# Attention by pairs of heads: half-array matmuls, probabilities divided before the transposes

## What is computed

```
def attend(q, k, v, scale):
    s = jnp.einsum('bhqd,bhkd->bhqk', q, k).astype(jnp.float32) * scale
    p = jax.nn.softmax(s, axis=-1).astype(v.dtype)
    return jnp.einsum('bhqk,bhkd->bhqd', p, v)
...
        s_win = jnp.einsum('bhqd,bhrkd->bhqrk', q_row, k_band).astype(f32) * scale + bias
        s_ctx = jnp.einsum('bhqd,bhcd->bhqc', q_row, kc).astype(f32) * scale
```

## Time and profile before

| | us |
|---|---|
| median of 3 runs | 1773.76 |
| lowest and highest | 1771.92, 1777.18 |
| the profiled execution, whole | 1772.61 |
| its span on the core | 1770.9 |

### The profile page before, as it was taken

One profiled execution on the slowest core, in us unless ns is written; L12 is line 12 of the kernel. 1 busy time (PEld: TensorE's weight loads), 2 busy tenths in 40 slices (PEclk: granted clock), 3 DMA queues, 4 the chain that ended last, 5 costly groups with the idle time before them and its releaser, 6 DMA issues.

```text
span 1770.9 us, 24625 instructions
## 1 busy us (share of the span) xinstructions
PE 1637.0 (92%) x9536; PEld 1383.1 (78%) x9536; DVE 992.3 (56%) x1739; ACT 759.2 (43%) x1470; POOL 670.4 (38%) x389
## 2 busy tenths in 40 slices
PE   7998989899999989899999998978899988889998
PEld 3876769766877668688888886967897876789998
DVE  5855825855275545359596964134136385546655
ACT  4333654344544443442323234247444644454443
POOL 0532334611343002355454553534551551133442
...
GB/s 336 198 141 78 201 92 166 176 39 1 98 96 183 26 102 92 51 143 143 142 191 166 285 167 119 66 95 79 155 96 48 93 140 96 99 133 193 178 188 119
DMA packets 69851, 230.63 MB, mean 130 GB/s; under 512 B 18280, under 2 KB 24808, under 8 KB 56424
## 3 DMA queue, kind: packets, MB, share of 16 engines
...
HBM read 216.45 MB, written 12.58 MB: 129 GB/s over the span
## 4 chain that ended last, share of the span: by engine, by line
PE 74%; DVE 10%; ACT 7%; issue 3%; POOL 3%; DMA 1%; ACTq 0%; POOLq 0%; DVEq 0%; SPq 0%
PE bank L1747 37%; PE bank L1829 9%; PE bank L1785 8%; PE bank L1767 4%; PE bank L2114 4%; PE bank L2093 3%; PE bank L1811 2%; PE bank L2100 2%; ACT wH L776 2%; POOL wL L663 1%; DVE mjunk L1204 1%; PE bank L1978 1%; DVE arena L1275 1%; POOL wL L665 1%; DVE acc L1207 1%
## 5 line engine op out<-in xcount | busy, mean ns | idle before, releaser
L663 POOL TENSOR_TENSOR wL<-raw,wH 128x1280 fp32r<-128x1280 f32 (+3 forms) x146 | 302.7, 2073 | 556.4 <-ACT wH L776 556.4
L665 POOL TENSOR_TENSOR wL<-raw,wH 128x768 fp32r<-128x768 f32 (+3 forms) x198 | 329.1, 1662 | 368.2 <-ACT wH L776 368.2
L776 ACT ACTIVATE wH<-raw 128x768 fp32r<-128x768 f32 (+6 forms) x396 | 296.7, 806 | 395.6 <-PE bank L1747 295.5
L1747 PE MATMUL bank<-hH,wH 128*128 128x512 f32 (+1 forms) x720 | 248.8, 346 | 5.2 <-DVE wL L1189 3.2
L1747 PE MATMUL bank<-hH,wL 128*128 128x512 f32 (+1 forms) x720 | 245.5, 341 | 0.0
L1747 PE MATMUL bank<-hL,wH 128*128 128x512 f32 (+1 forms) x720 | 245.4, 341 | 0.0
L1747 PE MATMUL bank<-oH,wH 128*128 128x512 f32 (+1 forms) x576 | 196.6, 341 | 2.9 <-DVE oL L1611 2.9
L1747 PE MATMUL bank<-oL,wH 128*128 128x512 f32 (+1 forms) x576 | 195.3, 339 | 0.0
L1747 PE MATMUL bank<-oH,wL 128*128 128x512 f32 (+1 forms) x576 | 195.2, 339 | 0.0
L1207 DVE SCALAR_TENSOR_TENSOR acc<-acc,cb 128x1024 f32<-128x1024 f32 x88 | 168.7, 1930 | 2.5
L1747 PEld LDWEIGHTS bank<-hH,wH 128*128 128x128 f32 x720 | 137.3, 191 | 22.8 <-DVE wL L1189 3.8
...
## 6 DMA issues: line engine op xcount, KB each, us to landing
...
```

Of the source, the lines that this page charges most:

```text
L663: pool.tensor_tensor(l_[:, 0:cut], r_[:, 0:cut], h_[:, 0:cut].bitcast(F32), ALU.subtract)
L665: pool.tensor_tensor(l_[:, cut:k * w], r_[:, cut:k * w], h_[:, cut:k * w].bitcast(F32), ALU.subtract)\
L776: act.activation(flat(wH, n)[:, part], flat(raw, n)[:, part], ACT.Copy)\
L1747: ins = pe.matmul(dst, w_[:, kk, c:c + P], r_[:, kk, lo:TOK], start=kk == k0 and m == 0, stop=kk == k0 + kn - 1 and m == 2)
```

## The change

Two heads that stand side by side in one group of 128 features make one step: 16 steps in layer 0, 8 in layer 1, plus 2 to drain. For `na`, `a_q` is no longer padded: the scores of the even head use partitions 0 to 63 and those of the odd head 64 to 127, in pieces of 128 keys that alternate between the two heads and their banks 4 and 5. VectorE divides the probabilities in SBUF (`pn`) before they are transposed. Then the values are stationary (64 columns) and the transposed probabilities move, so that the output comes out feature by token, the two heads in the two halves of the partitions of one bank; the transposes of the output, `s_o` and its division are gone. ScalarE rounds each pair's 128x128 output to `oH`, and VectorE writes `oL`. Probabilities have four buffers. The biases of the 512-key `na` scores are added in one instruction, with 256 zeros for the context keys. The scores of the next pair wait for the maximum where the scores were moved to SBUF (`na`, 512 keys), otherwise for Exp. Side work is spread anew by `side_done`, its last 12 matmuls in the first draining step. The first `na` block of each layer becomes `SHARED`. GpSimd's memset before the `na` phase is 256 wide instead of 4096. In the diff the three old loops (lines 1067 to 1099, 1575 to 1618 and 2079 to 2129 above) are left out, as are some old lines that one new line replaces.

```diff
+def head_pairs(l):
+    return [(qi, t, g) for qi, t in enumerate(att_tiles(l)) for g in range(HEADS // 2)]
...
+        a_q, a_k, a_v, a_tb = view(0, 4, TOK), view(2048, 4, TOK), view(4096, 4, 512), view(8192, 8, 6, 64)
+        A_ZERO, A_TB = 7936, 8192
...
+        s_pt = view(13824, 2, 512)
+        s_probs = dict(na=[view(at, 512) for at in (6144, 6656, 7168, 12800)],
+                       mla=[view(at, 512) for at in (12800, 13312, 10240, 10752)])
...
+        SHARED = [name in ("to", "wo") or (name == "ml" and j < 2) or (name, j) == ("na", 0) or (name, l) == ("ff", 1) for name, l, j in KEYS]
...
+        def side_done(br, l, s):
+            n = len(head_pairs(l))
+            if br == "na" and s == 0:
+                return 0
+            return KC * 12 if s >= n else (KC - 1) * 12 * (s + 1) // n
+        def side_step(br, l, c):
+            return next(s for s in range(len(head_pairs(l)) + 1) if side_done(br, l, s) >= 12 * c + 12)
...
-                pool.memset(a_q, 0.0).then_inc(S(f"na{l}_zero").handle, 1)
-                low_to(reach(N["ns", l, KC - 1]))
-                low_to(reach(N["ms", l, KC - 1]))
+                pool.memset(view(A_ZERO, CTX), 0.0).then_inc(S(f"na{l}_zero").handle, 1)
+                for br, last_used, side_name in (("na", ("na", l, 5), "ns"), ("mla", ("gate", l, GATES - 1), "ms")):
+                    low_to(reach(N[last_used]))
+                    turns = head_pairs(l)
+                    for s in range(len(turns) + 2):
+                        for c in range(KC):
+                            if side_step(br, l, c) + 1 == s:
+                                low_to(reach(N[side_name, l, c]))
+                    end()
...
-                            act.wait_ge(*S(tag + "zero").at(1))
-                            for up in range(2):
-                                r = slice(64 * up, 64 * up + 64)
-                                for tt in range(ntl):
-                                    src = tb[r, tt * 256:tt * 256 + 256].rearrange("p (a t) -> p a t", a=2)
-                                    dst = a_q[r, h0 + up:h0 + 4:2, (t + tt) * P:(t + tt) * P + P]
-                                    ins = act.activation(dst, src, ACT.Copy, scale=gcols[r, 0:1])
+                            for tt in range(ntl):
+                                src = tb[:, tt * 256:tt * 256 + 256].rearrange("p (a t) -> p a t", a=2)
+                                dst = a_q[:, h0 // 2:h0 // 2 + 2, (t + tt) * P:(t + tt) * P + P]
+                                ins = act.activation(dst, src, ACT.Copy, scale=gcols[:, 0:1])
...
+                    turns = head_pairs(l)
+                    for s in range(len(turns) + 2):
+                        if s >= 2:
+                            _, t, g = turns[s - 2]
+                            act.wait_ge(*S(tag + "o").at(s - 1))
+                            act.activation(oH[:, (4 if br == "na" else 0) + g, t * P:t * P + P], bank[s % 2][:, 0:P], ACT.Copy)\
+                                .then_inc(S(tag + "oH").up(1), 1)
+                        if 1 <= s <= len(turns):
+                            nk = att_keys(turns[s - 1][1]) * P
+                            for i in range(2):
+                                k = 2 * s - 2 + i
+                                act.wait_ge(*S(tag + "pt").at(k + 1))
+                                if s >= 2:
+                                    act.wait_ge(*S(tag + "o").at(s - 1))
+                                act.activation(s_pt[:, i, 0:nk], bank[6 + i][:, 0:nk], ACT.Copy).then_inc(S(tag + "pts").up(1), 1)
+                        if s < len(turns):
+                            qi, t, g = turns[s]
                             nk = att_keys(t) * P
+                            for i in range(2):
+                                k = 2 * s + i
+                                probs = s_probs[br][k % 4][:, 0:nk]
+                                act.wait_ge(*S(tag + "max").at(k + 1))
+                                if k >= 4:
+                                    act.wait_ge(*S(tag + "pt").at(k - 3))
+                                act.activation(probs, probs if br == "na" and t >= 2 else bank[4 + i][:, 0:nk], ACT.Exp,
+                                               bias=stat[:, 16 + k % 4:17 + k % 4],
+                                               accum_out=stat[:, 20 + k % 4:21 + k % 4]).then_inc(S(tag + "p").up(1), 1)
                         for c in range(KC):
+                            if side_step(br, l, c) + 1 == s:
                                 ahead(N["ns" if br == "na" else "ms", l, c])
...
+                share_ahead(N["gate", l, gate_range(l, "last").stop - 1])
...
+                    turns = head_pairs(l)
+                    def attended(s):
+                        if s >= 2:
+                            _, t, g = turns[s - 2]
+                            c, cols_ = (4 if br == "na" else 0) + g, slice(t * P, t * P + P)
+                            dve.wait_ge(*S(tag + "oH").at(s - 1))
+                            dve.tensor_tensor(oL[:, c, cols_], bank[s % 2][:, 0:P], oH[:, c, cols_].bitcast(F32),
+                                              ALU.subtract).then_inc(S(tag + "oL").up(1), 1)
+                    for s in range(len(turns) + 2):
+                        for k in (2 * s - 2, 2 * s - 1) if 1 <= s <= len(turns) else ():
+                            dve.wait_ge(*S(tag + "p").at(k + 1))
+                            link(dve.reciprocal(stat[:, 24 + k % 4:25 + k % 4], stat[:, 20 + k % 4:21 + k % 4]))
+                            probs = s_probs[br][k % 4][:, 0:att_keys(turns[s - 1][1]) * P]
+                            dve.tensor_scalar(probs, probs, stat[:, 24 + k % 4:25 + k % 4], None, ALU.mult)\
+                                .then_inc(S(tag + "pn").up(1), 1)
+                        for c in range(KC):
+                            if side_step(br, l, c) + 1 == s:
+                                branch_out(br, l, c)
+                            if br == "mla" and c < KC - 1 and side_step(br, l, c) + 2 == s:
+                                share_ahead(N["ms", l, c])
+                        for i in range(2 if s < len(turns) else 0):
+                            qi, t, g = turns[s]
+                            k, h, nk = 2 * s + i, 2 * g + i, att_keys(t) * P
+                            src = bank[4 + i][:, 0:nk]
+                            dve.wait_ge(*S(tag + "s").at(k + 1))
+                            if k >= 4:
+                                dve.wait_ge(*S(tag + "p").at(k - 3))
                             if br == "na" and t >= 2:
+                                if k >= 4:
+                                    dve.wait_ge(*S(tag + "pt").at(k - 3))
+                                step = A_TB + (h * 6 + (2 if t == 2 else 0)) * GRID_W - A_ZERO
+                                bias = view(A_ZERO, 2, step)[:, :, 0:CTX]
+                                scores = s_probs[br][k % 4]
+                                link(dve.tensor_tensor(scores.rearrange("p (a w) -> p a w", a=2),
+                                                       src.rearrange("p (a w) -> p a w", a=2), bias, ALU.add))
+                                src = scores
+                            dve.reduce_max(stat[:, 16 + k % 4:17 + k % 4], src, axis=AX,
+                                           negate=True).then_inc(S(tag + "max").up(1), 1)
+                            if i == 0:
+                                attended(s)
+                        if s >= len(turns):
+                            attended(s)
...
+                    turns = head_pairs(l)
+                    for s in range(len(turns) + 2):
+                        if s < len(turns):
+                            qi, t, g = turns[s]
+                            if s:
+                                moved = br == "na" and turns[s - 1][1] >= 2
+                                pe.wait_ge(*S(tag + ("max" if moved else "p")).at(2 * s))
                             if br == "na":
+                                for c in range(att_keys(t)):
+                                    for i in range(2):
+                                        r = slice(64 * i, 64 * i + 64)
+                                        ins = pe.matmul(bank[4 + i][:, c * P:c * P + P], a_q[r, g, t * P:t * P + P],
+                                                        a_k[r, g, c * P:c * P + P], start=True, stop=True)
+                                        if c == att_keys(t) - 1:
+                                            ins.then_inc(S(tag + "s").up(1), 1)
                             else:
+                                for i in range(2):
+                                    nk = att_keys(t) * P
+                                    pe.matmul(bank[4 + i][:, 0:nk], l_q[0:MLA_D, 2 * g + i, t * P:t * P + P],
+                                              l_k[0:MLA_D, 2 * g + i, 0:nk], start=True, stop=True).then_inc(S(tag + "s").up(1), 1)
+                        if s >= 2:
```

(21 more changed lines are left out.)

136 lines of the change are left out of this document (8 added, 128 removed).

## The result

| | before | after |
|---|---|---|
| median of the first comparison, us | 1773.99 | 1726.58 |
| lowest and highest of the four runs | 1771.92, 1777.18 | 1723.77, 1731.03 |
| the profiled execution, and its span | 1772.61, 1770.9 | 1731.03, 1729.3 |

The ratio is .9734, 95% interval .9708 to .9759: some 47 us less. In a second comparison, with five runs, it was .9731 (.9717 to .9744), 1729.15 against 1776.83. The profiled execution is 4.4 above the median of the first, so terms read from its trace add up to -41.6 and not to -47.4.

What follows compares the result with a forecast made beforehand. It took the Exp-to-Exp periods of the four attention loops as the bound, TensorE having no gap with 512 keys. Loops, ends and the rest summed to -45.8 from 1772.6, giving 1727 us; own range 1712 to 1739, 8 in 10 1708 to 1768.

Steps and rivals of the forecast that it cites:

- loops, layer 0: neighbourhood, latent: First to last Exp in layer 0: neighbourhood 86.9 to 65.2 us (-21.7), latent 83.8 to 75.3 (-8.5).
- loops, layer 1: neighbourhood, latent: First to last Exp in layer 1: neighbourhood 47.7 to 37.4 us (-10.3), latent 48.2 to 43.0 (-5.2).
- end of latent, layer 1: Stretch after layer 1's last latent Exp: 7.15 us becomes 10.4, +3.2, through a late gate tile.
- first projection, two layers: Wait for GpSimd before each layer's first projection shrinks by 2.35 us, -4.7 in all.
- Periods: Exp-to-Exp time per head pair: latent 6.2 us with 512 keys, 3.7 with 256; neighbourhood 5.1 to 5.2 and 3.4.
- The unknown price: Half-array matmul in scores and values: taken as .067 us side by side, 1.07 for 16 values; 1.71 in a row.
- the array empties at each change of shape: Rival, chance .12: TensorE drains when matmul shape changes, .2 us each, 120 changes, +24 us, 1751.
- One after the other: Rival, chance .22: half-array matmuls in the attention loops run in sequence, 16 values 1.71 us, scores 1.82; total 1755.
- The late gate tile: Layer 1's latent end: gate tile load queued behind the first wo block, which waits for VectorE's weight share; landing 5.1 us.
- The share on VectorE: First neighbourhood weight block: VectorE takes part of GpSimd's conversion, so the second piece starts 2.35 us earlier per layer.
- VectorE-bound: Neighbourhood pairs with 512 keys: VectorE, without gaps, sets the period of 5.1 to 5.2 us.
- The clock: Rival, chance .08: TensorE gaps within attention pairs bring the lower clock, 1.2 GHz; 130 us for all 48 pairs, 1857.

Runs made afterwards that it cites:

- The kernel that is this rival: Changed kernel with neighbourhood scores and all loops' values issued head by head, not alternating between array halves: 1741.96 us, ratio .9804.

## Why the prediction was right, and where it was not

**The sum.** 1727 against 1726.58 (1729.15 later). The terms, from the profiled executions:

| term | forecast | measured |
|---|---|---|
| loops, layer 0: neighbourhood, latent | -21.7, -8.5 | -21.4, -10.7 |
| loops, layer 1: neighbourhood, latent | -10.3, -5.2 | -11.5, -4.5 |
| end of neighbourhood, layer 0 | +1.0 | +1.4 |
| end of latent, layer 1 | +3.2 | +5.5 |
| other two ends | 0 | -.2 |
| first projection, two layers | -4.7 | -1.4 in each |

The last Exp to the first projection took 6.3 in place of 4.9 at the first end, 12.6 in place of 7.15 at the second. The measured terms make -44.2 of the profiled -41.6. The other 2.6 is not in any of them, nor were the query copies (-1.6) and the weight conversions behind Exp (+2) taken apart.

The mechanisms came as forecast, but that the sum hits to within 1 us is in part luck: the loops gave 2.4 more than forecast (-48.1 for -45.7), the ends and the first projection 4.4 less (+3.9 for -.5), and the profiled execution is itself 4.4 above the median. The working has three slips that changed nothing: 7 x 3.4 + 8 x 5.2 is 65.4 and not 65.2, 7 x 3.7 + 8 x 6.2 is 75.5 and not 75.3, and the terms of the latent end make 10.65 and not 10.4.

**Periods: right.** 6.11 for 6.2, 3.74 for 3.7, 3.33 for 3.4. Neighbourhood with 512 keys came to 34.2/7 = 4.9 on average in layer 0 and 5.0 in layer 1 for 5.1 to 5.2 (the expectations above have 5.09, which counts the two Exps of a pair into it), but my one number hides four cases: 4.5 without a side tile, 5.0 with one (4.7 in layer 1, where a tile is half as wide), 5.8 and 6.2 where GpSimd is in the way, and 5.7 in the second pair of layer 1, where TensorE makes up the side work of two pairs.

**The unknown price: right in sum, wrong in its parts.** I took .067 for a half-array matmul, so 1.07 for 16, and gave the drain a chance of its own, .12, as something that would come on top of the forecast or not. Measured are 1.02 for the values, and they hold both: 16 x .053 = .85, the lower bound, and .17 of drain; on the way into them scores lose another .2. So "I take .067" was too dear by .2 a pair, and "the array empties at each change of shape" was true, at .17 and not .2, though nowhere shown by the rows of before: the change from 128 to 64 stationary columns in the earlier trace rows has no gap, and I let it speak against the drain. Two errors of .2 to .4 a pair cancelled.

**One after the other: right for one half, wrong between the two.** The rival's 1755 went by 1.71 for sixteen values and 1.82 for sixteen scores. The kernel that is this rival ran at 1741.96, with 1.34 and 1.44 (1.51 and 1.64, less the gap at the change). The .107 was right for one half (.109 measured); what failed in "one after the other they go by their 128 moving columns, .107 each" is "one after the other", since the second half's instructions began four places early. With 256 keys that covers the whole row, so the rival's 4.0 and 4.1 were 3.75 and 3.34; with 512 its 6.8 and 5.85 were 6.59 and 5.3 to 5.5.

**The late gate tile: right, too small.** Its place in the queue was as told. The block in front of it waited for VectorE's share as I had it, but then .6 us more for GpSimd's part of the same weight block, which ends at 1472.49. Of the 12.6 us, 3.9 lie before the tile's issue (I had 4.35), 1.3 behind its landing (1.2). The term that was mis-sized is "landing 5.1": from 1473.27 to VectorE's start at 1480.68 it took 7.4, 2.3 more than in the earlier trace rows.

The block of weights in front is not the reason, though I took it for one: the tile stood behind it in the earlier trace rows too (issued at 1514.29 and 1514.72), and in layer 0 of the changed kernel, where it landed in 5.1. What differs is ScalarE's load of 1024 KB. It was issued at 1516.63 in the kernel before, behind both; now it is under way first, since the tile has moved behind it:

```profile
arena<-g_spill SPq DMA_DIRECT2D x1, 128.0 KB, 5.0
...
arena<-g_spill SPq DMA_DIRECT2D x1, 128.0 KB, 7.3
```

(kernel before, changed kernel; size, us to landing.) In the nine profiles that have the tile behind the block, it landed in 5.6 to 7.5 us in layer 1, with this load first, and in 4.9 to 5.4 in layer 0, with this load last. No run moved this load alone, so the reason is read from rows and not shown by an edit.

The clock behind the wait needed no term: in the kernel before, the first 4 us of `wo` were granted .50 too, and from the first `wo` matmul to the end both kernels took 247.3.

```profile
1523.65:1527.65 4.00, 4.00 (x19) 4.00 (x20) 1.98 (x5) 2.00 (x7) 0.00 (x0) 0.50 0.02 4
```

**The share on VectorE: too large.** "The second piece starts some 2.35 earlier" nearly held: counted from ScalarE's first conversion it started at 2.08 (258.38 - 256.30) instead of 4.19 (260.79 - 256.60), 2.11 earlier. The step that failed is that the share costs GpSimd nothing: the piece took 2.48 in place of 1.81, beside VectorE's share. 2.11 - .67 = 1.44, which is what the wait lost. The last line is of the kernel before:

```profile
256.30 2.00 ACT L789 ACTIVATE wH<-raw 128x1280 fp32r<-128x1280 f32 x2 [0.46 <-ACT gst L818]
...
257.70 1.49 DVE L1198 TENSOR_TENSOR wL<-raw,wH 128x1280 fp32r<-128x1280 f32 x1 [4.10 <-ACT wH L789]
...
258.38 2.48 POOL L675 TENSOR_TENSOR wL<-raw,wH 128x768 fp32r<-128x768 f32 x1 [24.28 <-ACT wH L789]
...
261.11 0.35 PE L1841 MATMUL bank<-wH,hH 128*128 128x256 f32 x1 [4.27 <-POOL wL L675]
...
260.79 1.81 POOL L665 TENSOR_TENSOR wL<-raw,wH 128x768 fp32r<-128x768 f32 x1
```

**VectorE-bound: nearly.** "VectorE sets the period" is true of its chain, not of its busy time: doubling the division cost half of what I expected in the regular pairs, and halving it gained nothing in half of them. **The clock** rival didn't come: the latent loops and the neighbourhood loop of layer 1 were granted .95 to 1.00, the 512-key part of the first loop 1.00; its 256-key part had .88, which is the long second pair told under the share.
